# Three attentions in a two-block transformer: outputs scaled after the value products, and the first block's queues in another order

## What is computed

```python
# window, sparse, causal:
p = softmax(s); o = einsum('bhqk,bkhd->bqhd', p, v)      # then o @ w_out
# full attention of the second block (mixer_b):
pr = softmax(sc); o = einsum('bkgqs,bksd->bkgqd', pr, v)
return (o * silu(gate)) @ w_out
```

## Time and profile before

| | us |
|---|---|
| median of 3 runs | 1089.21 (1088.77 to 1090.64) |
| the profiled execution | 1090.27 |
| its span, first to last instruction | 1088.4 |
| PE busy | 992.9 (91%) |
| DVE busy | 722.9 (66%) |
| ACT busy | 548.8 (50%) |
| mean granted TensorE clock | 0.964 of 2.4 GHz |

### The profile page before, as it was taken

One profiled execution on the slowest core, in us unless ns is written; L12 is line 12 of the kernel. 1 busy time (PEld: TensorE's weight loads), 2 busy tenths in 40 slices (PEclk: granted clock), 3 DMA queues, 4 the chain that ended last, 5 costly groups with the idle time before them and its releaser, 6 DMA issues.

```text
span 1088.4 us, 14619 instructions
## 1 busy us (share of the span) xinstructions
PE 992.9 (91%) x5660; PEld 807.2 (74%) x5660; DVE 722.9 (66%) x1133; ACT 548.8 (50%) x885; POOL 61.1 (6%) x47
## 2 busy tenths in 40 slices
PE   5897888999999989989899999988998999988995
PEld 2663467989898766767798989866886787767784
DVE  3497668777676586756875544686546587884475
ACT  3356625645363243654564545244665565647472
POOL 0000002300000000000440000000000000210000
PEclk9898989999999889999999999999999899998998
DMA  9748626889887466423798865544433165540040
GB/s 351 241 157 327 232 78 225 283 286 313 310 305 271 166 208 238 142 78 87 242 296 224 235 193 181 191 134 145 146 118 117 49 205 182 194 135 20 30 155 39
DMA packets 106931, 204.85 MB, mean 188 GB/s; under 512 B 3488, under 2 KB 37680, under 8 KB 106864
## 3 DMA queue, kind: packets, MB, share of 16 engines
q1 hardware_dynamic: 103808, 193.25, 53.0%
q0 software_dynamic: 3056, 10.67, 3.5%
HBM read 202.76 MB, written 1.15 MB: 187 GB/s over the span
## 4 chain that ended last, share of the span: by engine, by line
PE 62%; DVE 20%; ACT 9%; issue 6%; DMA 3%; SPq 0%; ACTq 0%; DVEq 0%
PE bank L1662 12%; PE bank L1664 11%; PE bank L1663 11%; PE bank L1716 5%; DVE w_lo L1828 5%; PE bank L1717 5%; PE bank L1718 5%; ACT w_hi L1281 3%; DMA raw<-in_ada_w 2%; PE bank L1791 2%; ACT probs L1475 2%; PE bank L1737 2%; PE bank L1759 2%; DMA raw<-in_mlp_w 1%; PE bank L1626 1%
## 5 line engine op out<-in xcount | busy, mean ns | idle before, releaser
L1828 DVE TENSOR_TENSOR w_lo<-raw,w_hi 128x2048 fp32r<-128x2048 f32 (+2 forms) x134 | 308.8, 2312 | 183.3 <-ACT w_hi L1281 182.1
L1281 ACT ACTIVATE w_hi<-raw 128x2048 fp32r<-128x2048 f32 (+2 forms) x134 | 248.3, 1857 | 131.0 <-PE bank L1664 69.7
L1662 PE MATMUL bank<-w_lo,ht_hi 128*128 128x512 f32 (+1 forms) x544 | 221.7, 407 | 15.4 <-DVE w_lo L1828 5.4
L1663 PE MATMUL bank<-w_hi,ht_hi 128*128 128x512 f32 (+1 forms) x528 | 208.1, 394 | 0.0
L1664 PE MATMUL bank<-w_hi,ht_lo 128*128 128x512 f32 (+1 forms) x528 | 208.0, 394 | 0.0
L1662 PEld LDWEIGHTS bank<-w_lo,ht_hi 128*128 128x128 f32 x544 | 105.2, 193 | 45.1 <-issue 18.4
L1716 PE MATMUL bank<-ht_hi,w_lo 128*128 128x256 f32 x448 | 127.6, 285 | 2.4 <-DVE w_lo L1828 2.3
L1717 PE MATMUL bank<-ht_lo,w_hi 128*128 128x256 f32 x448 | 126.8, 283 | 0.0
L1718 PE MATMUL bank<-ht_hi,w_hi 128*128 128x256 f32 x448 | 126.8, 283 | 0.0
L1664 PEld LDWEIGHTS bank<-w_hi,ht_lo 128*128 128x128 f32 x528 | 101.7, 193 | 21.8
L1663 PEld LDWEIGHTS bank<-w_hi,ht_hi 128*128 128x128 f32 x528 | 102.2, 194 | 19.6 <-issue 0.5
(11 more groups left out here) (236 smaller groups left out, 1353.3 us busy)
## 6 DMA issues: line engine op xcount, KB each, us to landing
raw<-in_mlp_w SPq DMA_DIRECT2D x64, 1024.0 KB, 5.9
raw<-in_ada_w SPq DMA_DIRECT2D x44, 1024.0 KB, 5.2
raw<-in_a_w_in SPq DMA_DIRECT2D x16, 1024.0 KB, 5.3
raw<-in_c_w_in SPq DMA_DIRECT2D x12, 1024.0 KB, 5.4
raw<-in_b_w_in SPq DMA_DIRECT2D x10, 1024.0 KB, 5.1
raw<-in_ple_w_gate SPq DMA_DIRECT2D x8, 1024.0 KB, 5.0
raw<-in_ab_w_in SPq DMA_DIRECT2D x4, 1024.0 KB, 9.8
tok<-in_ada_w SPq DMA_DIRECT2D x4, 1024.0 KB, 12.8
```

The lines of the kernel that those rows point to most:

```text
L1281: nc.scalar.activation(split_parts(n)[0], raw_tile(t), ACT.Copy).then_inc(high_done, 1)
L1662: nc.tensor.matmul(dst, a_hi[:, c, rows], lo[:, k, :], start=it["first"] and k == 0, stop=False)
L1663: nc.tensor.matmul(dst, a_hi[:, c, rows], hi[:, k, :], start=False, stop=False)
L1828: nc.vector.tensor_tensor(lo, raw_tile(split[n]), hi.bitcast(F32), ALU.subtract).then_inc(low_done, 1)
```

## The change

- Sparse and causal: the probabilities are turned unscaled. After the value product's bank is entered, four small products (the reciprocals rs, broadcast to 64 columns, times the identity) put the reciprocals, transposed, into the other half of the same bank. DVE copies that half to SBUF and multiplies the output by it into out_turned. DVE's four scalings of probabilities (L2314) and ACT's copy (L1489) are gone for these 12 pairs, `probs` waits for the exponentials alone, and `values` for the reciprocals.
- Full: the reciprocals are multiplied into the gate's columns in tok (item scale_gate, DVE), PE transposes these two tiles into bank 7, the values are made transposed as in the other modes, DVE copies the turned gates and multiplies the output by them. `gated`, the transposes of the output and their copies are gone for this attention; `split_out` takes their place.
- First block: the items are put in another order. The first weight tile's high part is split on ACT before the first half of x, the second half of x is split before the first block of low and its partner are all done, the searches for the keys come earlier among the window pairs, the window's last values and two modulation tiles go behind the first sparse scores, and the last modulation products, gate_row(0) and columns(1, 1) go behind the first piece of y[1].

```diff
--- before.py
+++ after.py
@@ -67,8 +67,11 @@
 BANDED = 4
 HIGH_SLOTS = 3
 UPDATED_BY_VECTOR = (1, 3)
-TURNED_OUT = ("window", "sparse", "causal")
+TURNED_OUT = ("window",)
+NORMED_OUT = ("sparse", "causal")
 NORMED_BY_SCALAR = ("window",)
+GATED_OUT = ("full",)
+GATE_COL = {"full": 1536}
 
 
 CONST = {}
@@ -305,12 +308,17 @@
                 held[p]["scaled"] = True
 
         def probs(p):
-            if held[p]["mode"] in TURNED_OUT:
+            if held[p]["mode"] in TURNED_OUT + NORMED_OUT:
                 scale(p)
+            if held[p]["mode"] in GATED_OUT:
+                add("scale_gate", mode=held[p]["mode"], g=g0 + p, p=p, scores=held[p]["banks"], heads=held[p]["heads"])
             add("probs", mode=held[p]["mode"], g=g0 + p, p=p, scores=held[p]["banks"], banks=banks((4, 5)))
 
+        def gate_bank(p):
+            return banks((7,)) if held[p]["mode"] in GATED_OUT else None
+
         def values(p, after=()):
-            return add("values", mode=held[p]["mode"], heads=held[p]["heads"], g=g0 + p, p=p, banks=banks((6,)), after=evicted(*after),
+            return add("values", mode=held[p]["mode"], heads=held[p]["heads"], g=g0 + p, p=p, gate=gate_bank(p), banks=banks((6,)), after=evicted(*after),
                        turned=evicted(next(i for i in plan if i["kind"] == "probs" and i["g"] == g0 + p)))
 
         return scores, probs, values, scale
@@ -544,6 +552,7 @@
     early = [job("turn_early", (4 + 2 * half, 5 + 2 * half), src="x", a=4 * half, n=4, dst="ht", wait=0,
                  affine=("early", half + 1)) for half in range(2)]
     early = [{**it, "turned": True} for it in early]
+    add("next_high", until=0)
     split_rows("x", KD, "ht", 0, ("early", 1), turned=early, halves=(0,))
     add("first_split")
     w = R["ab_w_in"][0]
@@ -555,19 +564,21 @@
     low(0, 0, ts=(0,))
     early_product(0, 1, 4, 2)
     early_product(1, 1, 0, 3)
-    low(0, 1, ts=(1,))
-    add("next_split", until=2)
     early_product(1, 1, 4, 3)
     early_columns(0, 1, 4)
     early_columns(1, 1, 5)
-    keys(0, 1)
+    low(0, 1, ts=(1,))
+    keys(0, 0)
+    add("next_high", until=2)
     split_rows("x", KD, "ht", 0, ("early", 2), turned=early, halves=(1,))
+    add("next_split", until=2)
     low = low(1, 2)
     add("rope_tables")
     add("rope", what=[(512, 2, 2304, HD)], rows=rows(), after=evicted(low))
     ak_rows = count["rows"]
+    keys(1, 1, ts=(0,))
     split_rows("cq", 2, "plt", 0, ("vec", VEC_B["q_norm"]), halves=(0,), after=evicted(low), pairs=(4, 5))
-    keys = keys(1, 2)
+    keys = keys(1, 2, ts=(1,))
     add("rope", what=[(1024, 2, 2560, P)], rows=rows(), after=evicted(keys))
     key_rows = count["rows"]
     biq = opened(R["ab_w_uiq"][0], 0, 512, 2, "plt", ("tok", 1792, 1.0, 512), (0, 1))(0, 1)
@@ -591,7 +602,7 @@
     index(0, left)
     index(1, (4, 5))
     index(2, left)
-    aq(1, 1, ts=(0,))
+    aq(1, 0, ts=(0,))
     index(3, (4, 5))
     aq = aq(1, 1, ts=(1,))
     bq = opened(R["ab_w_uq"][0], 0, 512, 2, "plt", ("tok", 1280, ("cq", 0), 512), right)(0, 0)
@@ -600,57 +611,62 @@
     ada_tiles(2, 7)
     add("topk", first=0)
     aq_turned += turn_all([0, 128, 256, 384], 0, evicted(aq), aq_rows, (4, 5))
-    scores(0, aq_turned, left)
-    ada_tiles(1)
+    scores(0, aq_turned, left, late=None)
     scores(1, [], right, late=None)
     ada_tiles(1)
+    scale(0)
     add("topk", first=4)
-    scale(0)
     scores(2, [], left, late=None)
     probs(0)
-    ada_tiles(1, 7)
     scale(1)
+    add("topk", first=8)
+    ada_tiles(1)
+    values(0, (low,))
     scores(3, [], right, late=None)
-    values(0, (low,))
+    probs(1)
+    scale(2)
     add("rope", what=[(1280, 8, None, HD)], rows=rows(), after=evicted(bq))
     bq_rows = count["rows"]
-    probs(1)
-    ada_tiles(1)
-    scale(2)
     values(1)
     probs(2)
+    bq_turned = turn_all([1280, 1408, 1536, 1664], 8, evicted(bq), bq_rows, left)
     scale(3)
-    add("topk", first=8)
-    bq_turned = turn_all([1280, 1408, 1536, 1664], 8, evicted(bq), bq_rows, left)
+    add("topk", first=12)
     values(2)
+    ada_tiles(1, 7)
     probs(3)
-    add("topk", first=12)
-    ada_tiles(1)
-    o_last = values(3)
+    prepare(1)
     ada_tiles(1)
     y = [opened(R["ab_w_out"][0], n * 512, 512, KD, "ht", ("y_ln", n, 0), (2 * n, 2 * n + 1)) for n in range(2)]
     scores(4, key_turned + bq_turned, left, late=None)
-    scores(5, [], right, late=True)
+    scores(5, [], right, late=None)
+    o_last = values(3)
+    ada_tiles(1)
+    scale(4)
+    ada_tiles(1)
+    scale(5)
+    probs(4)
+    split_out(0, o_last)
+    scores(6, [], right, late=None)
+    columns(1, 0, (6,))
+    probs(5)
+    values(4, (low, keys))
+    y[0](0, 1, ts=(0,))
+    scores(7, [], right, late=None)
+    scale(6)
+    values(5)
+    probs(6)
+    y[0](0, 1, ts=(1,))
     ada_tiles(1, 7)
-    columns(1, 0, (6,))
-    split_out(0, o_last)
-    prepare(1)
+    scale(7)
+    values(6), probs(7)
     ada_tiles(1)
-    probs(4)
-    scores(6, [], left)
-    ada_tiles(1)
-    values(4, (low, keys)), probs(5)
-    scores(7, [], right)
-    ada_tiles(1)
-    values(5), probs(6)
-    y[0](0, 1, ts=(0,))
-    values(6), probs(7)
-    columns(1, 1, (7,))
-    gate_row(0, (6, 7))
-    y[0](0, 1, ts=(1,))
     o_last = values(7)
     y[1](0, 1, ts=(0,), look=4)
     split_out(1, o_last)
+    ada_tiles(2)
+    gate_row(0, (6, 7))
+    columns(1, 1, (7,))
     y[1](0, 2, ts=(1,))
     last_tiles(0)
     mlp(0, None)
@@ -723,6 +739,9 @@
         y = [opened(w, n * 512, 512, KD, "ht", ("y_rms", n), (2 * n, 2 * n + 1)) for n in range(2)]
 
         def split(half):
+            if i:
+                split_out(half, o_last[half])
+                return
             rows_of_half = first_gated if i == 0 and half == 0 else gated(half, col)
             split_rows("o", KD, "ht", 0, halves=(half,), after=("gated", rows_of_half["n"]))
 
@@ -850,7 +869,9 @@
     scores(3, [], (0, 1)), values(1), probs(2)
     turn_two(6)
     scores(4, [turned[4]]), values(2), probs(3)
-    scores(5, [], (0, 1)), values(3), probs(4)
+    scores(5, [], (0, 1))
+    o_last = {0: values(3)}
+    probs(4)
 
     def after_full(y, split):
         split(0)
@@ -859,7 +880,7 @@
         scores(7, []), values(5), probs(6)
         values(6), probs(7)
         y[0](0, 1, ts=(1,))
-        values(7)
+        o_last[1] = values(7)
         y[1](0, 1, ts=(0,))
         split(1)
         y[1](0, 2, ts=(1,))
@@ -1049,6 +1070,8 @@
         probs_turned = sem("probs_turned")
         head_out = sem("head_out")
         sums_turned = sem("sums_turned")
+        gates_scaled = sem("gates_scaled")
+        gates_turned = sem("gates_turned")
         normed = sem("normed")
         gate_done = sem("gate_done")
         index_scores = sem("index_scores")
@@ -1765,7 +1788,20 @@
                     enter(it["after"])
                     enter(it["banks"])
                     b, _ = it["banks"][0]
-                    if mode in TURNED_OUT:
+                    if mode in GATED_OUT:
+                        pe.wait_ge(gates_scaled, it["p"] + 1)
+                        enter(it["gate"])
+                        col = GATE_COL[mode] + P * it["p"]
+                        for t in range(T):
+                            mm = nc.tensor.transpose(bank[it["gate"][0][0]][:, t * P:(t + 1) * P], tok[:, t, col:col + P], ident)
+                        mm.then_inc(gates_turned, 1)
+                    if mode in NORMED_OUT:
+                        pe.wait_ge(sums_turned, it["g"] + 1)
+                        for t in range(T):
+                            for j in range(2):
+                                nc.tensor.matmul(bank[b][j * HD:(j + 1) * HD, S + t * P:S + (t + 1) * P],
+                                                 rs[:, it["g"] % PAIRS_HELD, t, j:j + 1].broadcast_to([P, HD]), ident, start=True, stop=True)
+                    if mode in TURNED_OUT + GATED_OUT + NORMED_OUT:
                         for s, used in it["turned"]:
                             pe.wait_ge(bank_free[s], used)
                         for k in range(T):
@@ -2305,7 +2341,7 @@
                     if mode == "window":
                         link(nc.vector.tensor_tensor(sums[:, r, :, :], sums[:, r, :, :], sink_exp[:, r, :, :], ALU.add))
                     nc.vector.reciprocal(rs[:, r, :, :], sums[:, r, :, :]).then_inc(sums_turned, 1)
-                    if mode in NORMED_BY_SCALAR:
+                    if mode in NORMED_BY_SCALAR + NORMED_OUT:
                         continue
                     dve.wait_ge(sums_turned, g + 1)
                     for j in range(2):
@@ -2314,7 +2350,34 @@
                             ins = nc.vector.tensor_scalar(rows, rows, rs[:, r, t, j:j + 1], None, ALU.mult)
                         ins.then_inc(normed, 1)
 
-                elif kind == "values" and it["mode"] not in TURNED_OUT:
+                elif kind == "scale_gate":
+                    g, col = it["g"], GATE_COL[it["mode"]] + P * it["p"]
```

(26 more changed lines are left out.)

## The result

Before, the median was 1089.21 us; the changed kernel's was 1079.11 (1075.20 to 1081.16, five executions), a ratio of 0.9899 (95% interval 0.9868 to 0.9929). Measured again beside the last experiments it was 1083.80 (1072.38 to 1087.99, twelve executions), ratio 0.9954 (0.9927 to 0.9981). The median of all seventeen is 1081.82. The forecast was 1082.5. A ratio is not the quotient of the two medians (0.9907 for the first comparison), and it leaves out two slow executions, one of e1 (2956.36) and one of the kernel before beside e1 to e4 (1926.07).

A forecast was written before the change was run, and what follows sets the result against it. PE was taken as the bound, with short hand-overs to ACT and DVE. First block -2.8, causal +3.1 and full -7.0 sum to -6.7: 1083.6 us for the profiled execution, 1082.5 for the median, range 1074 to 1090.5.

The forecast's parts named there:

- rival A: Half clock on PE after new waits in window pairs, modulation rows and full: sum +3, 1092.5 us; chance 0.13.
- Price of the products: Four reciprocal products on PE cost 0.58 us, bounds 0.47 and 0.87, as two heads' column halves overlap.
- Rival D: Column halves never overlap: products 0.94, full's values as now, 1091 us, or 1100 with weight loads in line; chance 0.04.
- Full, -7.0: Full attention: cheaper values, fewer transposes and waits give -9.2, two waits for ACT +2.2; bounds -3 and -9.
- ACT's pace: Full: ACT needs 3.4 us a pair; wait before pair 6's values grows 1.1, the same again for pairs 2 to 4.
- rival B: ACT keeps full's pace; only transposes and their waits are won beside 1 us: full -4, 1085.5 us; chance 0.17.
- The cover of bank 7: Full's new waits, on gates_scaled and bank 7's copy, cost nothing; without cover, about 1 us of DVE a pair.
- Causal, +3.1: Causal: six products on PE's queue 3.5, DVE-scaling wait of 1.33 goes, ACT's 2.06 stays, DVE tail +0.9.
- First block, -2.8: Start to second half of y: 152.6 us against 155.4; bounds -8 and +5.
- The walk: Window pairs, step by step: values(0) and scores(3) done at 98.3 us, sparse scores at 111.3, 3.4 earlier.
- the start-up: First block's opening: PE's waits shrink by 1.4 us at 45 us, of which 0.65 is passed on.
- Rivals C and E: C: first block and full -8 each, 1076 us, chance 0.13. E: edits don't tell, 1088 us, chance 0.07.

The follow-up runs named there:

- e1: Kernel before with only full's part of the change: 1079.44 us, ratio to the kernel before 0.9907 (0.9885 to 0.9928).
- e4: Kernel before with only the first block's new order, sparse probabilities still scaled by DVE: ratio to the kernel before 1.0015 (0.9997 to 1.0034).
- e3: Kernel before with the first block's new order and the sparse products, causal and full as before: ratio to the kernel before 0.9991 (0.9968 to 1.0013).
- e5: Changed kernel with the sparse and causal reciprocal products repeated, ordered by head, and full's values ordered by head: 1086.25 us in one execution.
- e6: Changed kernel with full's queries 4 and 5 turned ahead of scores(2): ratio to the kernel before 0.9952 (0.9927 to 0.9977).
- e12: The changed kernel measured again, nothing altered: 1083.80 us, ratio to the kernel before 0.9954 (0.9927 to 0.9981).
- e11: Changed kernel with the split of the last query piece's weights asked for one step earlier again: ratio to the kernel before 0.9927 (0.9896 to 0.9957).
- e7: Changed kernel with the second modulation row's columns in bank 5 instead of bank 7: ratio to the kernel before 0.9886 (0.9843 to 0.9929).

## Why the prediction came out as it did

The sum was -6.7 in three terms, -2.8, +3.1, -7.0. By stretches they are nothing that can be shown (means +1.0, e3's times -1.0), +1.9, and -8.3 by the means or -9.3 in the profiled pair. That the median came out near the forecast is in good part luck: a gain that did not come is made up by a smaller loss and a larger gain. In the recorded text the sum of rival A is off by 0.3: its 9.7 on top of the forecast give 1092.2.

**Price of the products.** Taken 0.58, bounds 0.47 and 0.87; measured 0.66 with drain, 0.49 to the next start (137.39 to 137.88). The size was right, its reason not: I read the factor 0.62 as the overlap of two heads in two column halves. e5 puts the products of one head behind each other, and they take the same. All that the runs show is that such records, with 64 columns of weights, are cheap in either order. Rival D fell with its price (0.94, or 1.9 and more for full's values). The gates' two transposes, put at 0.2, take 0.37 to the next start (994.23 to 994.60). The Trainium skill, TensorE: Matmul & The Clock Gate, "Part 3: Packing small matmuls", lets a weight load overlap running products only where the row group differs. The time of 1100 that I put beside it did not come, and as the order by head changes nothing, e5 shows neither an overlap nor its absence. The record has one row that an account of these prices must also fit, the modulation's products, which go into four quarters of 32 columns in turn:

```profile
110.41 1.06 PE L1585 MATMUL bank<-raw,cs 128*32 128x512 f32 x8
```

The next record starts at 111.41: 4096 column steps in 1.00 us, 1.7 for each pulse of a clock granted at 2.4 GHz. Something runs side by side there; no experiment took it apart.

**Full, -7.0: measured -9.3 in the profiled pair, -8.3 by the means of seven and four executions.** Starts of the values behind the cut, before and after:

```
pair      1     2     3     4     5     6     7     end
before   33.4  40.6  44.7  51.0  57.6  61.7  68.7  131.4
changed  35.3  39.9  43.4  47.5  53.7  57.8  62.8  122.1
```

The forecast, cut at the same places, is -3.7 up to pair 4's values, -0.4 from there to pair 7's, and -2.9 behind them. Measured are -3.5, -2.4 and -3.4. Up to pair 4 two errors cancel. Pair 1 is 1.9 later (the 4.84, costed at nothing). From pair 1 to 4 the gain is 5.4 and not 3.7: the half clock that stood on pair 1's values and the transposes behind them (3.64 and 1.92, now 1.21 and 1.09) now stands on scores(3) before them. The 1.1 that I had put there for ACT's pace is in the waits, 0.58 and 0.53, where before had none; it is outweighed. From pair 4 to 7 the term for ACT's pace was wrong: the wait before pair 6's values grew by 0.4 (0.87 + 0.68 against 1.14) and not by 1.1. Before, that wait was also followed by half clock, on transposes and a piece of y, which the change spares. Behind pair 7 come the shorter values, the second transposes and the 1.39. The gains without ACT's term were 9.2, and that 9.3 was measured is no proof of them: e3, with the old code in full, has no half clock behind pair 6 and takes 129.5 and not 131.4.

ACT is 3.4 a pair in both, as I had it (2.30 + 1.09), but the pairs already followed each other at 4.0 where nothing lay between (997.6 to 1001.6), now at 3.5 to 4.1; DVE's maxima and the hand-overs are part of the pace. That is rival B's fall too; its second half, little gained from the values themselves, is true of pairs 2 and 3.

**The cover of bank 7.** I costed the new waits at nothing and put the risk at 1 us for a pair. A wait of 4.84 came, at a place I had not named: not at the gates but at the turning of queries, which uses the same bank. It takes the place of the 3.37; turning the queries earlier gives back 0.8 to 2.2 (e6). The step missed that an instruction's bank has other users further down PE's queue.

**Causal, +3.1: measured +1.9.** The wait of 1.33 went, the 2.06 stayed (2.13), the tail cost 0.7 of the 0.9. What was mis-sized is the products. By the starts of the values behind the cut (before and changed: 38.7 and 38.5, 47.2 and 47.5, 54.3 and 55.1, 62.85 and 62.6, 78.0 and 78.3, 82.05 and 82.4, 86.4 and 87.2, 90.8 and 92.0) those of pairs 1, 2, 6 and 7 add about 0.45 each, pair 3's some 0.3 beside the 1.33 that goes and pair 4's 0.6, while pairs 0 and 5 add nothing. Pair 5's falls into a wait of 0.89 for ACT that is gone. So six do stand on PE's queue, though not the six I named, and they cost about 2.7 and not 3.5.

**First block, -2.8.** The sparse scores were to come at 111.3. They came at 113.2, in e12 with the same code at 113.5, and in others with this start-up at 112.8 to 115.8. The walk had values(0) and scores(3) done at 98.3; they started within 0.6 of it, but ran at half clock until 100.7. The rows, and PE's clock behind them:

```profile
96.39 1.55 PE L1812 MATMUL bank<-probs_t,tok 128*64 128x256 f32 x8 [2.67 <-ACT probs_t L1531]
...
98.92 1.22 PE L1760 MATMUL bank<-qkt 64*128 64x256 f32 x4
```

```profile
100.00:108.00 8.00, 5.01 (x26) 3.85 (x25) 7.11 (x21) 5.09 (x18) 0.00 (x0) 0.50 0.00 0
```

So the exponentials and all behind them came 2.2 later. This is rival A in small: the new order makes waits of 2.67 and 2.99, and PE's clock is 0.50 from 96 us to 109. The second step that failed is the start-up: I had it passing on 0.65 for sure, and did not see the new wait at 77 us, which comes from the one number of e11. With it mended the sparse scores came at 111.0, in the one execution there is. The sparse part held: 3.68 gone, 0.76 and 1.51 in the places named, and from the sparse scores to the first MLP 57.6 against 57.7. The half clock behind the 1.51, expected at 2.0 us, is not in this execution and is in e12 (about 1.6 us of time). Since the first block's length differs by 3 us between executions of like code, its sum stays open: the times give e3 -1.0, with an interval from -3.5 to +1.4, the stretches +1.0.

**Rivals C and E.** The first block did not give all its waits back, and the edits do tell, full's down and causal's up.

## What to carry to other kernels

When executions of one kernel spread by more than an edit is worth, cut every trace at the same few instructions and compare the stretches: here that gave causal's 1.9 us within some 0.3, one outlier of 1.5 aside, where the times gave 1.4 with an interval of 4. Look at the clock in each stretch too, since one more fall to half clock costs as much as such an edit. A product taken off PE's queue counts, but one that is added where the queue waits anyway may cost nothing, so add up by position and not by number. And before a bank is given a second use, look for who asks for it next on every queue.

## What was not expected of the hardware

- The spread of a kernel's time sits in PE's granted clock. The same 1288 records took 207.1 us at a mean of 0.99 and 214.3 at 0.96. And the clock falls there without any wait of PE. In the middle of this MLP, between split products that follow each other without a gap, stand two groups of 32 records with one moving column each. The second group and the clock behind it, in e6 and in e7:

```profile
354.57 4.56 PE L1597 MATMUL bank<-consts,late_sum 128*128 128x1 f32 x32
...
357.00:363.70 6.70, 6.70 (x22) 5.73 (x22) 0.67 (x4) 0.00 (x0) 0.00 (x0) 0.50 0.33 130
```

```profile
349.77 3.63 PE L1597 MATMUL bank<-consts,late_sum 128*128 128x1 f32 x32
...
350.00:378.00 28.00, 25.99 (x139) 20.01 (x138) 19.60 (x45) 7.88 (x12) 0.00 (x0) 1.00 0.59 204
```

All fourteen executions fall to half clock at the first group or just behind it, twelve also at the second. The two that do not, the changed kernel and e7, have the shortest first MLP (208.4 and 207.1; the twelve 209.9 to 214.3). By the granted clock of its windows e6 spends some 17 us of this stretch at half clock and e7 3.4; half of the difference, 6.8, is nearly all of the 7.2 between them. Why one execution falls and another does not was not tested.
- Plain float32 products get cheaper with the part of the array that their weights fill. 2048 column steps take 1.71 us to the next start with 128x128 weights (a gate row, 415.87 to 417.58 in the changed kernel), 1.02 with 128x64 (full's values, 994.60 to 995.62), in either order, and 1.06 with 64x128 (full's scores, 996.64 to 997.70); 4096 steps take 1.00 with 128x32 (the modulation).
- A wait of 1.9 us is followed by half clock in some executions of the same code and not in others (four of eight at 77 us), so the price of such a wait has two values: 1.9, or some 4 (an estimate from window scores at 83.6 to 83.9 and at 85.3 to 86.1).
